# A two-block network on one core: first loads in smaller pieces, the latent heads' outputs laid out by token, and one modulation sum three slots later

## What is computed

```python
y = x32 * rsqrt(mean(x32 * x32)) * g                 # first norm; p = y @ w_in
sh1, sc1, g1, ... = split(silu(c) @ w_ada + b_ada)   # modulation, 6 x 2048 columns
csh1, csc1, ...   = split(silu(c_ctx) @ w_ada + b_ada)
# per head, tokens i of a chunk of 64, both directions summed:
o = tril(q e^(a-mid) . k e^(mid-a)) @ v + (q e^a) @ S_start
o = o * rsqrt(mean(o*o over the 128 channels) + eps) * gain   # readout
```

## Time and profile before

| | us |
|---|---|
| median of 3 runs | 2660.53 |
| the profiled execution, its own time | 2664.66 |
| its span in the trace | 2662.9 |
| PE busy | 2631.2 |
| DVE busy | 1854.5 |
| ACT busy | 1338.8 |
| granted TensorE clock, mean over the span | 0.996 |

### The profile page before, as it was taken

The page is one execution under the profiler, slowest core; times in us unless marked ns, Lnnn a source line. Parts: engine busy times, 40 slices in busy tenths (PEclk is TensorE's granted clock), DMA queues, the critical chain, the costliest instruction groups (busy, mean ns, idle before and its releaser), DMA issues.

```text
span 2662.9 us, 42405 instructions
## 1 busy us (share of the span) xinstructions
PE 2631.2 (99%) x17956; PEld 2396.3 (90%) x17956; DVE 1854.5 (70%) x2227; ACT 1338.8 (50%) x1774; POOL 279.7 (11%) x258
## 2 busy tenths in 40 slices
PE   9999999999999999999999999999999999999998
PEld 8788886998998988988999899999899898998997
DVE  5555666799999777787678866677655685446555
ACT  5454454554444444466774345666454444443443
POOL 1232321010000000000010211110000000000011
PEclk9999999999999999999999999999999999999999
DMA  9545553568777788876566744445657785555553
GB/s 300 169 154 159 157 175 135 200 249 298 269 285 284 279 310 294 292 269 195 168 214 238 269 131 145 143 143 206 215 184 248 254 301 205 190 189 190 190 182 119
DMA packets 289260, 572.32 MB, mean 215 GB/s; under 512 B 9718, under 2 KB 32529, under 8 KB 288624
## 3 DMA queue, kind: packets, MB, share of 16 engines
q1 hardware_dynamic: 283376, 548.69, 60.5%
q0 software_dynamic: 5696, 20.92, 2.7%
HBM read 565.78 MB, written 3.27 MB: 214 GB/s over the span
## 4 chain that ended last, share of the span: by engine, by line
PE 95%; DVE 2%; ACT 1%; issue 1%; POOL 0%; ACTq 0%; DVEq 0%; POOLq 0%
PE p_gemm L2172 51%; PE p_gemm L2221 32%; PE p_gemm L2198 3%; PE p_b L2389 1%; DVE w_lo L1258 1%; PE p_b L2420 1%; PE p_b L2586 1%; PE p_b L2652 1%; PE p_b L2595 1%; PE p_b L2250 1%; PE p_b L2482 1%; ACT w_hi L701 0%; PE p_b L2296 0%; PE p_gemm L2191 0%; PE p_b L2403 0%
## 5 line engine op out<-in xcount | busy, mean ns | idle before, releaser
L1258 DVE TENSOR_TENSOR w_lo<-w_raw,w_hi 128x1024 fp32r<-128x1024 f32 (+2 forms) x872 | 1067.1, 1228 | 692.6 <-ACT w_hi L701 691.5
L701 ACT ACTIVATE w_hi<-w_raw 128x1024 fp32r<-128x1024 f32 (+2 forms) x872 | 899.1, 1033 | 1187.9 <-PE p_gemm L2172 670.1
L2172 PE MATMUL p_gemm<-h_hi,w_hi 128*128 128x256 f32 x2928 | 831.9, 284 | 3.5 <-DVE h_lo L1348 1.6
L2172 PE MATMUL p_gemm<-h_lo,w_hi 128*128 128x256 f32 x2928 | 824.2, 281 | 0.0
L2172 PE MATMUL p_gemm<-h_hi,w_lo 128*128 128x256 f32 x2928 | 824.2, 281 | 0.0
L2172 PEld LDWEIGHTS p_gemm<-h_hi,w_hi 128*128 128x128 f32 x2928 | 553.6, 189 | 12.7 <-issue 8.2
L2172 PEld LDWEIGHTS p_gemm<-h_lo,w_hi 128*128 128x128 f32 x2928 | 553.8, 189 | 0.9
L2172 PEld LDWEIGHTS p_gemm<-h_hi,w_lo 128*128 128x128 f32 x2928 | 553.4, 189 | 0.0
L2221 PE MATMUL p_gemm<-w_hi,a_hi 128*128 128x512 f32 (+1 forms) x1056 | 405.1, 384 | 0.1
L2221 PE MATMUL p_gemm<-w_hi,a_lo 128*128 128x512 f32 (+1 forms) x1056 | 404.3, 383 | 0.0
L2221 PE MATMUL p_gemm<-w_lo,a_hi 128*128 128x512 f32 (+1 forms) x1056 | 404.1, 383 | 0.0
(11 more groups left out here) (413 smaller groups left out, 2488.5 us busy)
## 6 DMA issues: line engine op xcount, KB each, us to landing
w_raw<-in_w_mlp SPq DMA_DIRECT2D x124, 1024.0 KB, 5.2
w_raw<-in_w_in SPq DMA_DIRECT2D x107, 1024.0 KB, 5.4
ada_w<-in_w_ada SPq DMA_DIRECT2D x96, 1024.0 KB, 6.1
w_raw<-in_w_up SPq DMA_DIRECT2D x64, 1024.0 KB, 8.8
w_raw<-in_w_down SPq DMA_DIRECT2D x64, 1024.0 KB, 9.6
w_raw<-in_w_out SPq DMA_DIRECT2D x32, 1024.0 KB, 5.1
w_raw<-in_w_in SPq DMA_DIRECT2D x36, 768.0 KB, 4.6
cmp_w<-in_phi_w POOLq DMA_DIRECT2D x2, 2048.0 KB, 16.0
```

The source lines that it names most:

```text
L701: act.activation(WH[:, s % 4, :, 0:n], RAW[:, s // 2, 2 * (s % 2):2 * (s % 2) + 2, 0:n], ACT.Copy)\
L1258: dve.tensor_tensor(WL[:, s % 4, :, 0:n], RAW[:, s // 2, 2 * (s % 2):2 * (s % 2) + 2, 0:n], WH[:, s % 4, :, 0:n].bitcast(F32), ALU.subtrac ...
L2172: ins = pe.matmul(dst, w[:, s % 4, kk, cols], x[:, k, :], start=k == 0 and m % 2 == 0 and i == 0, stop=k == KC - 1 and i == 2, skip_group_ ...
```

## The change

1. **Start.** SP loads the 16 gain columns alone (`prm[:, 0:16]`), the identity and 256 columns of `x`, all on one semaphore `first_loaded`; then the first half of the weights, the next 256 columns of `x`, the second half. The rest of `prm` follows behind the second piece of `x`. POOL loads the table's inputs only when `w_loaded0` is there. PE makes 8 products of ones, turns group 0, makes 3 more, turns group 1, and starts slot 0 with the 16 products that need only `w_hi`; the 8 with `w_lo` follow. Group 2 is turned behind slot 0. The table product moves to slot 5 on PE and its addition to slot 7 on DVE, the exponential of `c` behind slot 3 on ACT.
2. **Modulation.** For `B_CTX` alone, all three steps come three slots later.
3. **Latent heads.** Scores and values change sides, and so do states and queries, so that the outputs lie token by channel. The states' products have 64 stationary columns and fill rows 0 to 63 or 64 to 127 of the bank. ACT sums the squares while it squares, and logarithm and exponential work on 128 x 2 values. DVE scales by token behind slot 1 (`lat_scale`), PE turns the result behind slot 4 (`lat_turn`), DVE multiplies the gain in behind slot 5 (`lat_out`). PE's sum of squares is gone.

```diff
+ADA_LATE = {B_CTX: 3}
 # SP
-sp.dma_start(PR[:, :], a["prm"]).then_inc(S("prm_loaded"), 16)
-sp.dma_start(IDN[:, :], a["ident"]).then_inc(S("ident_loaded"), 16)
+sp.dma_start(prm("g_mix_pre", 0, 16), a["prm"][:, 0:16]).then_inc(S("first_loaded"), 16)
+sp.dma_start(IDN[:, :], a["ident"]).then_inc(S("first_loaded"), 16)
+sp.dma_start(X[:, :, 0:T], x_tok[:, :, 0:T]).then_inc(S("first_loaded"), 16)
...
+                        sp.dma_start(RAW[:, 0, 0:2, :], src[:, 0:2, :]).then_inc(S("w_first"), 16)
+                        sp.dma_start(X[:, :, T:2 * T], x_tok[:, :, T:2 * T]).then_inc(S("x_loaded0"), 16)
+                        sp.dma_start(RAW[:, 0, 2:4, :], src[:, 2:4, :]).then_inc(S("w_loaded0"), 16)
 # POOL
+            pool.wait_ge(S("w_loaded0"), 16)
             for dst, name in ((ONEHOT, "onehot"), (TADD, "tab_add"), (REL, "rel_bias")):
 # ACT
-            act.wait_ge(S("prm_loaded"), 16)
-            act.activation(TINY[:, 64:96], prm("c", 0, 32), ACT.Exp, scale=-1.0).then_inc(S("exp_c"), 1)
+            act.wait_ge(S("first_loaded"), 48)
             round_gain(0, 0, "g_mix_pre")
...
-                act.activation(OSQ[:, :], PB[1][:, 0:T], ACT.Square).then_inc(S("hg_osq"), 1)
+                for tb in range(2):
+                    ins = act.activation(OSQ[:, P * tb:P * tb + P], PB[1][:, P * tb:P * tb + P], ACT.Square, accum_out=HSS[:, tb:tb + 1])
...
-                act.activation(ORS[:, :], PB[2][:, 0:T], ACT.Ln, bias=prm("eps"), scale=1.0 / P).then_inc(S("hg_oln"), 1)
+                act.activation(HRS, HSS, ACT.Ln, bias=prm("eps"), scale=1.0 / P).then_inc(S("hg_oln"), 1)
...
                 if s == 0:
                     gate_log(0)
+                    lat_log(HG - 1)
                     gate_sigmoid(0)
-                if s == 1:
-                    lat_log(HG - 1)
                     lat_rstd(HG - 1)
 # DVE
-                if s == 1:
+                if s == ADA_LATE.get(b, 0) + 1:
                     ada_rest(b)
...
+            def lat_scale(h):
+                dve.wait_ge(S("hg_ors"), h + 1)
+                for tb in range(2):
+                    ins = dve.tensor_scalar(ON[:, tb, :], PB[1][:, P * tb:P * tb + P], HRS[:, tb:tb + 1], None, ALU.mult)
+                ins.then_inc(S("hg_out"), 1)
             def lat_out(h):
-                dve.wait_ge(S("hg_ors"), h + 1)
+                dve.wait_ge(S("hg_oturned"), h + 1)
...
+                dve.tensor_scalar(dst, ps, prm("hg_norm", h), None, ALU.mult).then_inc(S("hg_out"), 1)
...
                         if s == 1:
                             lat_decays(h)
+                            if h > 0:
+                                lat_scale(h - 1)
-                        if s == 3 and h > 0:
+                        if s == 5 and h > 0:
                             lat_out(h - 1)
 # PE
+                    if b == 0 and s == 0:
+                        pe.wait_ge(S("hi_ready"), 1)
...
+                if b == 0 and s == 0:
+                    for m in range(n):
+                        for i, x in enumerate((top, rest)):
+                            pe.matmul(gview(0)[:, m, :], WH[:, 0, kk, P * m:P * m + P], x[:, k, :],
+                                      start=k == 0 and m % 2 == 0 and i == 0, stop=False, skip_group_check=True)
+                    if kk == 1:
+                        pe.wait_ge(S("lo_ready"), 1)
...
-            pe.wait_ge(S("ones_ready"), 2)
-            keep_busy(1, 13)
-            pe.wait_ge(S("ident_loaded"), 16)
-            for j in range(3):
-                turn_first(j)
+            pe.wait_ge(S("ones_ready"), 1)
+            keep_busy(1, 8)
+            pe.wait_ge(S("first_loaded"), 48)
+            turn_first(0)
+            keep_busy(2, 3)
+            turn_first(1)
...
-                if s == 0:
+                if s == 5:
                     tables()
...
-                        if s == ADA_AT:
+                        if s == ADA_AT + ADA_LATE.get(b, 0):
                             ada_total(b)
...
-                        pe.matmul(PB[1][:, P * i:P * i + P], HVN[:, i, :], SCT[:, z, i, :], start=first, stop=False, skip_group_check=True)
+                        pe.matmul(PB[1][:, P * i:P * i + P], SCT[:, z, i, :], HVN[:, i, :], start=z == 0 and i == 0, stop=False,
+                                  skip_group_check=True)
-                for z in range(2):
-                    for i in range(NCH):
+                for i in range(NCH):
+                    for z in range(2):
                         n = i if z == 0 else NCH - 1 - i
-                        ins = pe.matmul(PB[1][:, ts], state, QAQ[:, z, ts], start=False, stop=z == 1, skip_group_check=True)
+                        rows = slice(CHUNK * (n % 2), CHUNK * (n % 2) + CHUNK)
+                        cols = slice(P * (n // 2), P * (n // 2) + P)
+                        ins = pe.matmul(PB[1][rows, cols], QAQ[:, z, CHUNK * n:CHUNK * n + CHUNK], state, start=False, stop=True,
+                                        skip_group_check=True)
...
+            def lat_turn(h):
+                ps = bank(1, "hg_out", 2 * h + 2)
+                for tb in range(2):
+                    ins = pe.transpose(ps[:, P * tb:P * tb + P], ON[:, tb, :], IDN[:, :])
+                ins.then_inc(S("hg_oturned"), 1)
```

More of the change, by code:

```diff
@@ L316, in program @@
         OSQ = at("hg_osq", HB0 + 27 * K, [P, T])
-        ORS = at("hg_ors", HB0 + 28 * K, [P, T])
+        ON = at("hg_on", HB0 + 28 * K, [P, 2, P])
+        HSS, HRS = TINY[:, 42:44], TINY[:, 44:46]
         VMID = [HV, HX1, HX0]
@@ L842, in _ @@
                         round_gain(0, s + 3, "g_mix_pre")
+                    if s == 3:
+                        act.wait_ge(S("prm_loaded"), 16)
+                        act.activation(TINY[:, 64:96], prm("c", 0, 32), ACT.Exp, scale=-1.0).then_inc(S("exp_c"), 1)
                     if s == MIX_FIRST:
@@ L1349, in rest_mod, with silu_c @@
                    .then_inc(S("tok_lo"), 1)
[L1352 to L1357, removed]
+            def silu_c():
+                ec = TINY[:, 64:96]
+                dve.wait_ge(S("exp_c"), 1)
+                own(dve.tensor_scalar(ec, ec, 1.0, None, ALU.add))
+                own(dve.reciprocal(ec, ec))
+                own(dve.tensor_tensor(SIL[:, :, :].rearrange("p k z -> p z k"), ec.rearrange("p (z k) -> p z k", z=2),
+                                      prm("c", 0, 32).rearrange("p (z k) -> p z k", z=2), ALU.mult))
+            dve.wait_ge(S("first_loaded"), 48)
             rest_gain(0, 0, "g_mix_pre")
@@ L2019, in _ @@
                 ada_step(B_G + 1, s)
+                if s == 0:
+                    lat_scale(HG - 1)
                 if s == 3:
@@ L2164, in gemm_half @@
                         pe.wait_ge(*gemm_read(b - 2, g))
-                    pe.wait_ge(S("lo_ready"), count(b, g, UPB, s + 1))
+                    if b == 0 and s == 0:
+                        pe.wait_ge(S("hi_ready"), 1)
+                    else:
+                        pe.wait_ge(S("lo_ready"), count(b, g, UPB, s + 1))
                 k = 2 * s + kk
+                if b == 0 and s == 0:
[5 more added lines that the diff above has]
+                        pe.wait_ge(S("lo_ready"), 1)
+                        for m in range(n):
+                            for k in range(2):
+                                ins = pe.matmul(gview(0)[:, m, :], WL[:, 0, k, P * m:P * m + P], top[:, k, :], start=False, stop=False,
+                                                skip_group_check=True)
+                        ins.then_inc(S("unit_used"), 1)
+                    return
                 for m in range(n):
@@ L2448, in _ @@
                 half(1)
+                if s == 0:
+                    turn_first(2)
                 if s + 3 < 8:
                     turn_first(s + 3)
-                if s == 0:
+                if s == 5:
                     tables()
@@ L2670, in _ @@
                     else:
-                        if s == 0 and h > 0:
-                            lat_square_sum(h - 1)
+                        if s == 4 and h > 0:
+                            lat_turn(h - 1)
                         if s == 5:
@@ L2681, in _ @@
                 gemm_unit(B_G + 1, None, s, AH, AL)
-                if s == 0:
-                    lat_square_sum(HG - 1)
+                if s == 2:
+                    lat_turn(HG - 1)
             def gain_rows(n, section, m):
```

54 lines of the change are left out of this document (25 added, 29 removed).

## The result

The changed kernel takes 2664.86 us, the median of 20 runs (2663.56 to 2665.49); the kernel before, in 20 runs on the same chips, 2660.9 (2659.2 to 2664.66). The ratio is 1.0013, 95% interval 1.0007 to 1.0019: **slower by 3.5 us**, where 5.8 us of gain were forecast. That is within the bound of 0.2%, with an interval that leaves zero out, and 10 us off the forecast.

The account below looks back on a forecast made before the run. PE, busy 99% of the span, was taken to bound the kernel. Start -4.5, modulation -2.9 and latent heads +1.6 gave -5.8 us, from a median of 2660.53 to 2654.7; own range 2652.5 to 2657.

Parts of the forecast that it names:

- slot 2 at 17.9: Start on PE: slot 2 would begin at 17.9 us, where before it was 23.17, so 5.3 earlier.
- Gain 4.5: Start: 4.5 us gained, the later table product counted against 5.3; lower bounds 2.8 and 2.1, upper 5.2.
- The paragraph on DMA: Start's transfers: 0.33 MB ahead of the first group, 0.84 MB with half the weights, taken to land in time.
- the 1.76 for slot 0 at full clock: Start: share of the 4.5 us gain from slot 0 taking 2.84 us at full clock instead of 4.60.
- `B_CTX`, gain 2.9: Modulation sum three slots later: one pause split into four, 4.1 us together, no half clock; 2.9 us gained.
- +0.03 per head: Latent heads with a predecessor: net cost of squares gone, transposes, outputs and a wait, -0.42 + 0.22 - 0.29 + 0.52.
- Outputs -0.29: Latent heads' state products: 16 records in alternating halves take 1.42 us instead of 1.71, 12 at 0.107 plus 0.14.
- the rival of full overlap: Latent state products: halves run side by side, switching free, 0.4 us less in each of 8 heads, 2651.3; chance 17%.
- Wait 0.87: Latent heads: PE waits 0.87 us before the scores for `lat_out` on DVE; net +0.52 after 0.35 of slack.
- 1.5 behind head 7: `B_G + 1`: PE waits 1.7 us for the scaling before `lat_turn`, with -0.42 + 0.22 making +1.5.
- DVE in the latent blocks: Latent blocks: `lat_scale` waits for ACT's root, delaying later splits; seven waits grow by 1.9 each, 2668; chance 5%.
- The clock falls anyway: Half clock remains at the start (+1.7 us) and in `B_CTX` (+2); mean of the cases 2657.5; chance 22%.

Follow-up runs that it names:

- the early one: Start's edit with table product behind slot 1 on PE, addition behind slot 2 on DVE, against the kernel before: 2664.42 us; with bias loads moved too, 2657.69.
- the second profile: The kernel before, unchanged, run and profiled once more: 2660.45 us, span 2658.7.

## Why the prediction was wrong

**Slower by 3.5, forecast faster by 5.8.** By its own steps:

- *Start, "slot 2 at 17.9".* The local working held: ones to 6.9 (forecast 7.2), table load 1.28 behind `turned`, first activation right behind its end at 8.87, slot 0 at 10.80 (10.9), slot 2 at 17.79 (17.9). Slot 3 then came 0.5 late (21.60) behind a weight transfer that landed at 18.4, so 3.65 of the 4.5 were there at 47 us (47.05 to 43.40).
- *"Gain 4.5", carried whole into the sum.* **This is the step that failed.** The paragraph on DMA priced transfers for the first 10 us, where 0.84 MB counted, and put POOL's later loads at "nothing": it asked when the table's inputs are wanted, and not what POOL issues behind the table's result, 2 + 2 MB and the bias. What the runs showed in its place is a start that cannot be fed up to 76 us: the start's edit by itself cost 3 us, with ACT held 6.3 to 6.9 us for a weight piece ahead of its roots, a wait of 5.6 to 6.5 (2.5 before) and half clock behind it. Of the two candidates the bias loads weigh most: moving them gains 5.0 us with the late table and 6.7 with the early one. The late table, which the prediction put at nothing, costs nothing that shows while the bias loads are in front (2664.5 and 2664.42) and 1.8 without them, inside the noise. With both amended, 3.2 of the 4.5 came through. That PE comes out later than before, and not only equal, lies in the bytes that come later than they did (21.4 MB for 23.3) and in the clock; why the queues carry less is open.
- *What the 4.5 was measured against.* Eight of the profiles have the old start. In four of them (both of the kernel before are among these) slot 0 ran at half clock, and the place at 47.05 above lies at 46.2 to 47.1; in the other four it ran at full clock, at 43.9 to 44.7. The nine profiles with the new start have it at 42.3 to 44.6. So the 1.76 for slot 0 at full clock is often there already in the old start, and the new start is some 3 us ahead of one kind and 1 of the other.
- *The reference point.* That the profiled execution stood 4.1 above the median was taken as a constant to subtract. By the second profile 2.1 of it were half clock at 80 to 85 us, and 1.0 a longer half clock behind the modulation sum, which part 2 counts as gain as well: that 1.0 is subtracted twice. Behind the pause at `proj` the clock fell for the whole stretch in one of the eight profiles with the old start, for a part in three and not in four. In the three kernels with the new start and all loads in their way it fell each time. The profile of before lay at the upper end of its runs and that of after at the lower end; that is why the spans fell by 1.1 and the medians rose by 3.5 to 4.
- *`B_CTX`, gain 2.9.* Right within what can be told: 2.9 measured (interval 0.3 to 4.8), 3.2 and 2.0 in the traces, by which profile of before is taken. The mechanism too, four pauses (0.56, 0.86, 0.46, 1.27 for 0.75, 1.1, 0.75, 1.5) and the clock kept up.
- *Latent heads, +0.03 per head.* Right by two errors that cancelled. "Outputs -0.29" was -0.69: the rival of full overlap was the true one, 8 units and 0.17. "Wait 0.87" was 1.05 to 1.2: from the first decay to the split ahead of `lat_out` it is 12.3 us (1669.60 to 1681.93) where I had 12.0. One of the decays' subtractions takes 0.83 instead of 0.42; ACT releases POOL's `hg_k` earlier, so that it now falls on that subtraction (1672.24, where before it began 0.3 ahead of the decays' end). That POOL is what slows DVE there, and that ACT is earlier because it is rid of its passes over 256 columns, was read from the timelines, not tested. Blocks came to +0.1 and, with the strided heads, +0.3. The 1.5 behind head 7 were 1.4. (The part's own terms, +0.2, -0.3, +0.3 and +1.5, sum to 1.7, not 1.6.)
- *The rival that ended on the slower side* was DVE in the latent blocks, worth +13 with 5%. The loss came from another place; no rival had POOL's loads in it.
- *"The clock falls anyway", 22%.* Not in the start nor in `B_CTX`, where it was expected, but at 80 us, which the prediction did not look at.

## What to carry to other kernels

When a step is moved, follow its result to the end of what it releases, queue by queue: an early small product may be the gate of megabytes, and the transfers' share over the whole time up to the next hard wait (here 98% to 76 us) is a warning that a start that is earlier may not be fed. What can wait, here 1 MB of bias read 70 us later, is then the first thing to move. A gain at the start is only a gain behind the next place where another chain ends last; look for that place before adding it up. And a profile that lies outside the median's spread has to be explained or taken again before it is used as the base of a sum.

## What the runs showed of the hardware

- Products with 64 stationary columns, written to the lower and upper half of the rows in turn, run side by side: 16 records of an fp32 product in 1.02 us for 1.71 with 128 columns, also where four records of one half follow one another; 1.51 if all of one half come first. The Trainium skill, "TensorEngine Tiling (Array Packing)", section "Performance Considerations", names the swap of stationary and moving side with 2x column tiling; the traces agree in part: 1.7 times as fast, 8 units of 0.107 and 0.17 over. Its "Key Properties" speak of a drain at a change of mode: between the first of these records and the next slot, whatever it costs is inside that 0.17.
- The clock fell behind one pause of 2.47 us and stayed up behind another of 2.46 at the same place of the same kernel. At that place it also fell for a part of the way behind 2.38 (bias moved, old start) and stayed up behind 2.38 (bias moved, new start): the length of the pause alone does not decide it. It stayed up behind four pauses of 0.5 to 1.3 within ten us.
- An activation starts right behind its table load, 7.58 + 1.28 to 8.87. "ScalarE: Activation LUTs" in the Trainium skill, section "What ACT_TABLE_LOAD costs", adds 1.38 us of drain to each switch; none shows here, with ACT idle before the load nor behind another activation (before ACT works to 1815.97, the load begins at 1815.99, the sigmoid at 1817.28).
- The same 1 MB of bias loads was free in one kernel and worth 6.7 us in another: moving it gained 0.7 (within noise) where PE was not early, and all of the loss where it was.
